# One matmul of 512 columns for two of 256 in two narrow feed-forward up stages

## The reference

```python
def conv_glu_ffn(n, w_up, conv_w, conv_b, w_down):
    s = n.shape[1]
    gate, up = jnp.split(n @ w_up, 2, axis=-1)
    gp = jnp.pad(gate, ((0, 0), (CONV_WIDTH - 1, 0), (0, 0)))
    conv = conv_b
    for j in range(CONV_WIDTH):
        conv = conv + gp[:, j:j + s] * conv_w[j]
    return (jax.nn.silu(conv) * up) @ w_down
```

## Time and profile before

| What | Value |
|---|---|
| Median of 3 runs | 1887.92 us (1886.67 to 1890.25) |
| Profiled execution, its own time | 1885.0 us |
| Its span in the trace | 1882.9 us |
| TensorE matmuls busy | 1773.3 us, 94% |
| VectorE, ScalarE, GpSimd busy | 717.8, 878.8, 948.0 us |
| Mean DMA rate | 140 GB/s |

### The profile page before, as it was taken

One profiled execution on the slowest core, in us unless ns is written; L12 is line 12 of the kernel. 1 busy time (PEld: TensorE's weight loads), 2 busy tenths in 40 slices (PEclk: granted clock), 3 DMA queues, 4 the chain that ended last, 5 costly groups with the idle time before them and its releaser, 6 DMA issues.

```text
span 1882.9 us, 26936 instructions
## 1 busy us (share of the span) xinstructions
PE 1773.3 (94%) x10762; PEld 1477.0 (78%) x10762; DVE 717.8 (38%) x1567; ACT 878.8 (47%) x1566; POOL 948.0 (50%) x416
## 2 busy tenths in 40 slices
PE   8999999997899999898998999999999898899998
PEld 6668998776699988775555788888888876679986
DVE  4443231344332353742557143343200453344421
ACT  4655454445555643433325354444422454456652
POOL 4645688774278884340105234444343341248876
PEclk9999999999999999998999999999999999999999
DMA  8336865443256653227875133333232430136654
GB/s 270 102 102 214 245 187 173 168 156 112 68 157 179 185 174 103 82 87 232 298 270 185 46 83 96 90 105 97 90 101 79 110 104 24 44 108 183 180 168 145
DMA packets 264846, 263.56 MB, mean 140 GB/s; under 512 B 11331, under 2 KB 202123, under 8 KB 264595
## 3 DMA queue, kind: packets, MB, share of 16 engines
q1 hardware_dynamic: 264435, 261.25, 44.9%
q10 hardware_dynamic: 288, 0.59, 0.1%
HBM read 260.76 MB, written 1.06 MB: 139 GB/s over the span
## 4 chain that ended last, share of the span: by engine, by line
PE 78%; DVE 8%; ACT 6%; DMA 5%; issue 2%; POOL 1%; SPq 1%; ACTq 0%; DVEq 0%
PE bank L370 22%; PE bank L371 21%; PE bank L372 21%; PE bank L1630 2%; PE bank L1251 2%; ACT work L1369 1%; ACT weights_high L357 1%; PE bank L1221 1%; DMA weights<-in_ada_w 1%; PE bank L918 1%; PE bank L2027 1%; PE bank L942 1%; DVE work L1330 1%; PE bank L585 1%; PE bank L1276 1%
## 5 line engine op out<-in xcount | busy, mean ns | idle before, releaser
L364 POOL TENSOR_TENSOR weights_low<-weights,weights_high 128x1024 fp32r<-128x1024 f32 (+1 forms) x388 | 919.1, 2385 | 771.4 <-ACT weights_high L357 770.7
L357 ACT ACTIVATE weights_high<-weights 128x1024 fp32r<-128x1024 f32 (+1 forms) x388 | 401.9, 1046 | 416.0 <-PE bank L372 120.6
L370 PE MATMUL bank<-normed_features_high,weights_high 128*128 128x256 f32 (+1 forms) x1408 | 437.6, 311 | 1.0 <-DVE normed_features_low L497 0.5
L371 PE MATMUL bank<-normed_features_high,weights_low 128*128 128x256 f32 (+1 forms) x1408 | 435.7, 309 | 0.0
L372 PE MATMUL bank<-normed_features_low,weights_high 128*128 128x256 f32 (+1 forms) x1408 | 435.7, 309 | 0.0
L370 PE MATMUL bank<-weights_high,normed_features_high 128*128 128x512 f32 (+4 forms) x752 | 289.1, 384 | 15.0 <-DVE big L748 7.2
L370 PEld LDWEIGHTS bank<-normed_features_high,weights_high 128*128 128x128 f32 x1408 | 268.7, 191 | 18.4 <-issue 3.3
L372 PEld LDWEIGHTS bank<-normed_features_low,weights_high 128*128 128x128 f32 x1408 | 268.7, 191 | 13.7
L371 PEld LDWEIGHTS bank<-normed_features_high,weights_low 128*128 128x128 f32 x1408 | 268.7, 191 | 13.6
L372 PE MATMUL bank<-weights_low,normed_features_high 128*128 128x512 f32 (+4 forms) x752 | 274.3, 365 | 0.0
L371 PE MATMUL bank<-weights_high,normed_features_low 128*128 128x512 f32 (+4 forms) x752 | 273.9, 364 | 0.0
(11 more groups left out here) (324 smaller groups left out, 2094.3 us busy)
## 6 DMA issues: line engine op xcount, KB each, us to landing
weights<-in_ffn_w_up SPq DMA_DIRECT2D x44, 1024.0 KB, 6.1
weights<-in_ffn_up SPq DMA_DIRECT2D x44, 1024.0 KB, 6.0
weights<-in_ada_w SPq DMA_DIRECT2D x40, 1024.0 KB, 6.5
weights<-in_ffn_w_down SPq DMA_DIRECT2D x20, 1024.0 KB, 5.1
weights<-in_ffn_down SPq DMA_DIRECT2D x20, 1024.0 KB, 5.1
weights<-in_diff_w_qkv SPq DMA_DIRECT2D x12, 1024.0 KB, 5.1
weights<-in_hyb_w_in SPq DMA_DIRECT2D x11, 1024.0 KB, 5.5
weights<-in_odd_w_in SPq DMA_DIRECT2D x9, 1024.0 KB, 5.3
```

The source lines that it names most:

```text
L357: A.eng.activation(high(whigh[:, m % HIGHS, :]), raw(wslot[:, u % SLOTS, :]), ACT.Copy).then_inc(scalar_done, A.one(("A", "high", m)))
L364: G.eng.tensor_tensor(raw(wlow[:, u % SLOTS, :]), raw(wslot[:, u % SLOTS, :]), high(whigh[:, m % HIGHS, :]).bitcast(F32), ALU.subtract).th ...
L370: T.eng.matmul(out_, lh, rh, start=first, stop=False)
L371: T.eng.matmul(out_, ll, rh, start=False, stop=False)
```

## The change

In 1.1 and 2.1 (now named in PAIRED) the features' high and low parts lie in one SBUF tensor, and one view takes the 256 high and 256 low columns of a k as a moving operand of 512 columns in two runs. The weights' high part is multiplied with both in one matmul: columns 0 to 255 of the bank get high x high, columns 256 to 511 high x low. A second matmul of 256 columns adds low x high to the first half of the bank. At the end of a chunk ScalarE copies columns 256 to 511 of each of the two banks into the unused half of cbuf's buffer, and VectorE adds the copy to the first half of the bank, before ScalarE's mid step may read it. VectorE's adds stand at the start of each f, in `up_V_causal` and in `up_V_both` alike, and its low part of the chunk before moves from behind the taps to just behind these adds. 1.1 leaves SHARED, so that it uses two banks per chunk, and its down stage now waits for the low part of chunk FC - 3 first. The number of matmul columns stays the same: 3 x 256 per product.

```diff
-        nt_high = sb("normed_features_high", KT * 512, F32R)
-        nt_low = sb("normed_features_low", KT * 512, F32R)
+        nt_both = sb("normed_features_high_low", 2 * KT * 512, F32R)
...
+        nTh = nt_both[:, 0:KT * 512].rearrange("p (k t) -> p k t", k=KT)
+        nTl = nt_both[:, KT * 512:2 * KT * 512].rearrange("p (k t) -> p k t", k=KT)
+        nTb = nt_both[:, :].rearrange("p (h k t) -> p h k t", h=2, k=KT)
...
-        SHARED = ("1.0 ffn up", "1.1 ffn up")
+        SHARED = ("1.0 ffn up",)
+        PAIRED = ("1.1 ffn up", "2.1 ffn up")
+
+        def aside_of(f, u, n):
+
+            b = (f % 2) * 3 + u
+            return qkt[:, b * 512 + n:b * 512 + 2 * n]
+
+        def up_product(T, ph, f, u, wh, wl, k, lo, n, first, last):
+
+            if ph not in PAIRED:
+                return product(T, up_bank(ph, f, u, n), (wh, wl), (nTh[:, k, lo:lo + n], nTl[:, k, lo:lo + n]), first, last)
+            bank = psum[2 * (f % 4) + u]
+            T.eng.matmul(bank[:, 0:2 * n].rearrange("p (h t) -> p h t", h=2), wh, nTb[:, :, k, lo:lo + n], start=first, stop=False)
+            return T.eng.matmul(bank[:, 0:n], wl, nTh[:, k, lo:lo + n], start=False, stop=last)
+
+        def whole_V(V, ph, f, n):
+
+            V.eng.wait_ge(tensor_done, done("T", ph, "up", f))
+            for u in range(2):
+                V.eng.wait_ge(scalar_done, done("A", ph, "aside", f, u))
+                V.eng.tensor_tensor(up_bank(ph, f, u, n), up_bank(ph, f, u, n), aside_of(f, u, n), ALU.add).then_inc(vector_done, V.one(("V", ph, "whole", f, u)))
...
-                            i = product(T, up_bank(ph, f, u, n), (wh[:, k, :], wl[:, k, :]), (nTh[:, k, lo:lo + n], nTl[:, k, lo:lo + n]),
-                                        k == 0 and (u == 0 or ph not in SHARED), k == KT - 1 and (u == 1 or ph not in SHARED))
+                            i = up_product(T, ph, f, u, wh[:, k, :], wl[:, k, :], k, lo, n,
+                                           k == 0 and (u == 0 or ph not in SHARED), k == KT - 1 and (u == 1 or ph not in SHARED))
...
-                        i = product(T, up_bank(ph, f, u, n), (wh[:, k, :], wl[:, k, :]), (nTh[:, k, lo:lo + n], nTl[:, k, lo:lo + n]), k == 0, k == KT - 1)
+                        i = up_product(T, ph, f, u, wh[:, k, :], wl[:, k, :], k, lo, n, k == 0, k == KT - 1)
...
                     A.eng.wait_ge(vector_done, done("V", ph, "product", f - 2))
+                for u in range(2 if ph in PAIRED else 0):
+                    A.eng.activation(aside_of(f, u, n), psum[2 * (f % 4) + u][:, n:2 * n], ACT.Copy).then_inc(scalar_done, A.one(("A", ph, "aside", f, u)))
                 for u in range(2 if both else 1):
+                    if ph in PAIRED:
+                        A.eng.wait_ge(vector_done, done("V", ph, "whole", f, u))
...
             for f in range(FC):
+                if ph in PAIRED:
+                    whole_V(V, ph, f, n)
+                    if f >= 1:
+                        up_low_V(V, ph, f - 1, n)
...
-                if f >= 1:
+                if f >= 1 and ph not in PAIRED:
                     up_low_V(V, ph, f - 1, n)
...
             elif up not in SHARED:
-                T.eng.wait_ge(vector_done, done("V", up, "low", FC - 3 if n > SEQ else FC - 2))
+                T.eng.wait_ge(vector_done, done("V", up, "low", FC - 2 if up == "2.1 ffn up" else FC - 3))
```

More of the change, by code:

```diff
@@ L194, in program @@
         xt = x_t[:, :].rearrange("p (t d) -> p t d", t=TT)
-        nTh = nt_high[:, :].rearrange("p (k t) -> p k t", k=KT)
-        nTl = nt_low[:, :].rearrange("p (k t) -> p k t", k=KT)
+        nTh = nt_both[:, 0:KT * 512].rearrange("p (k t) -> p k t", k=KT)
+        nTl = nt_both[:, KT * 512:2 * KT * 512].rearrange("p (k t) -> p k t", k=KT)
+        nTb = nt_both[:, :].rearrange("p (h k t) -> p h k t", h=2, k=KT)
         wslot = ring[:, :].rearrange("p (s n) -> p s n", s=SLOTS)
```

## The result

The changed kernel takes 1875.78 us (median of 10 runs, 1867.71 to 1882.18); the kernel before, run beside it, 1887.48 (10 runs, 1883.60 to 1897.21). The ratio is 0.9938, 95% interval 0.9916 to 0.9960: 11.7 us less, where 8.3 were forecast.

What follows compares the result with a forecast made beforehand. TensorE's matmul stream was taken as the bound in both up stages; -8.7 us from it and +0.4 at 2.1's end made -8.3, so 1887.9 became 1879.6 us (-0.44%), range 1876.5 to 1885.5.

Steps and rivals of the forecast that it cites:

- What bounds the kernel: Up stages of 1.1 and 2.1: TensorE never pauses at 2.4 GHz, so its instruction stream sets the time.
- The stream: TensorE in both up stages: product falls from 0.3600 to 0.3471 us, saving 12.9 ns each, 8.7 us in all.
- rival A: TensorE's up stages: the matmul's fixed part is not saved, or only partly; 1888.3, or 1884.0 if half stays; chance 0.13.
- The chain in 2.1: Hand-offs between ScalarE and VectorE in 2.1: turn grows from 4.9 to 5.56 us against TensorE's 5.55; nothing reaches TensorE.
- Rival B: 2.1's hand-off chain becomes the bound: 1880 to 1884, chance 0.10; slower than before by over 0.2%, chance 0.05.
- The end of 2.1: Start of 2.1's down stage after the last up matmuls: +0.4 us, between -0.5 and +0.6.
- a late DMA: Weights transfer in 2.1 taking 7.1 us, not 6.0: chain stays about 1.1 behind, down stage starts at T + 4.3.
- T + 3.2: End of 2.1: down stage starts 3.2 us after TensorE's chunk end T, if the chain is not behind; judged less likely.
- 1.1's end: 1.1's down-stage wait ends long before; context's turn pushed about 1.5 us into a room of 1.6: nothing, at worst 0.5.
- rival C: Down stages behind both up stages: freed time returns as waits for weights; about 1883 to 1887, chance 0.05.

Runs made afterwards that it cites:

- one_run: Changed kernel with each k's high and low feature parts stored adjacently, so the 512 columns are one run; stages 135.38 and 127.72 us, 0.3533 per product.
- long_chain: Changed kernel with two more ScalarE copies per chunk of 2.1; a chunk takes 6.12 us for 5.65, stage 2.1 8.1 us longer than 127.7.
- grouped: Changed kernel issuing four 512-column matmuls, then four of 256, in every chunk but the first; stages 134.55 and 126.88 us, 0.3508 per product.
- filled: Changed kernel with 21 unread 128-column matmuls at the start of 1.1's down stage; ratio 0.0055 below the previous kernel with the same matmuls.
- three: Changed kernel with the high weights meeting high and low parts in two 256-column matmuls again; ratio 1.0013 to the kernel before, stages 137.70 and 129.97 us.

## Why the prediction was right or wrong

*What bounds the kernel*: right. TensorE's stream sets both stages; leaving out the new work of the other engines gained nothing in 1.1, and taking out the 512-column matmul took back everything.

*The stream*: this is the first of the two steps that failed, and it was too large: 12.9 ns per product and 8.7 us were forecast, 6.7 ns and 4.6 us came in the traced execution. "I take 0.2271, the row with the same number of columns" was read from a row where 512 follows 512. In alternation a product takes 0.3533 in 9 stages of the 13 that keep one pace and 0.3467 in 4, so the gain is 2.3 us per stage (6.7 ns x 336 products) or, less often, 4.5. The reason given for the price that was missing, two runs of the moving operand, was wrong too: one_run has one run and the same time. It was in effect rival A's case of half the gain, by another mechanism. On average over the paces the stream gives 2 x (9 x 2.3 + 4 x 4.5) / 13 = 6.0 us.

The estimate of 1.7 us worked out from the Trainium skill, "TensorE: Matmul & The Clock Gate", section Back-to-back issue gap, does not agree with the traces: the stages give 4.6 us, 6.7 ns for each matmul dropped and not 2.5.

*The chain in 2.1*: right, 5.58 for 5.56, built from gaps of another kernel's turn. Rival B did not come; long_chain, where it does, has what the forecast named as its sign, TensorE's wait for weights_low. (By the forecast's own formula the change breaks even at a turn of 6.01, not 6.03.)

*The end of 2.1*: wrong in sign, small. Forecast +0.4, measured -0.9, or -1.1 if the means of all traces are taken (five with the old 2.1: 3.73, 3.51, 4.76, 5.16, 3.61, mean 4.2; seven with the new one: 2.87, 2.98, 3.00, 3.07, 3.44, 3.38, 2.97, mean 3.1). What failed is the premise that a late DMA comes: in six of the seven ScalarE was idle at most 0.41 us before a weights copy in the whole stage, so the other end, T + 3.2, was the right one. That a late DMA mostly stays is borne out by the seventh, grouped: there the copy waited 0.85 once, was then 1.51 behind TensorE's chunk, and made up 0.04 a chunk to 0.92 at the end. The largest values of the old order, 4.76 and 5.16, have a wait of ScalarE for the down stage's weights just there, 1.98 and 2.11; so 3.73 was a low draw, which the single trace could not tell.

*1.1's end and rival C*: right; the turn of the context comes with the stage, and the freed time isn't given back.

*The sum.* Stream 4.6 and tail 0.9 are 5.5, less than the 8.3; the kernel nevertheless gained 11.7 by the medians. At equal clock it is 8.2 with 1.2 to either side, and stream and tail in their means, 6.0 and 1.1, come to 7.1, within that. The rest, some 3 us, goes with a mean granted clock of 0.9808 for 0.9791 (1.7 x 1.64 = 2.8). This is the second step that failed: no term of the sum dealt with the clock, it was put at nothing without a reason. At equal clock the time would have been about 1887.5 - 8.2 = 1879.3, inside the range and near the forecast; the range missed the time because it had no such term. That the equal-clock figure, 8.2, meets the forecast's 8.3 is luck: the stream was forecast too large and the end of 2.1 with the wrong sign. Why the clock rises with the 512-column matmul stays open.

## What to carry to other kernels

Read the spacing of matmuls where the widths are mixed as they will be mixed: a stream that alternates 512 and 256 columns lost, in 9 stages of 13, about half of what fewer instructions should save, and eight of one width in a row took the saving per stage from 2.3 to 3.7 us. Before adding work to a chain of hand-offs, build one turn from the gaps of the trace; it came out to 0.02 us. And don't count a pause of TensorE by its length alone, since a longer one can be followed by a stretch at 1.2 GHz that costs as much again.

## What the runs showed of the hardware that was not expected

- The same stream of 512 and 256 columns runs at 0.3533 or 0.3467 us per product, 848 or 832 cycles of 2.4 GHz, and stays at it through 21 chunks; two executions of one kernel differ by it (135.40 and 133.15 us for stage 1.1). A short pause of TensorE can change it: in 1.1 of filled a product that started 0.22 late stood between the two paces.
- Groups of four give stages of 134.55 and 126.88, groups of eight 134.00 and 126.33, against 135.40 and 127.71 alternating at the slower pace; above 0.3471 per product that is 3.7, 2.0 and 6.2 ns for 8, 4 and 32 changes of width a chunk, so not one price per change.
- A moving operand in two runs, 4096 words apart, costs the same as one run.
- At the three places looked at, behind waits of TensorE of 1.89 us and more, matmuls ran at half the rate for 3 us and more in 10 of 12 cases (512 columns 0.43 us apart); behind those of 1.85 and less, in 2 of 20.
- 0.001 of the mean clock is worth 1.64 us in this kernel, and three and the changed kernel, which differ only in whether the high weights meet both parts in one matmul or in two, differ by 0.0024 in it (0.9784 over 12 runs, 0.9808 over 16; standard error of the difference 0.0009).
- At the start of 2.0's in stage TensorE waits 1.89 or 1.90 us in the six kernels without the copies and adds in 1.1, and 1.75 or 1.76 in the ten with them.
